# Gates of the first two mixers by exponential, addition and reciprocal in place of Silu, and the last outputs' turn three visits later

## What is computed

```python
def dsa_mixer(h, w_in, q_g, k_g, w_out):
    q, k, v, gate, qi, ki, wi = split_cols(h @ w_in, A_WIDTHS)
    q = rope(rms_norm(q.reshape(B, T, N_HEADS, HEAD_DIM), q_g), pos)
    k = rope(rms_norm(k.reshape(B, T, N_KV_HEADS, HEAD_DIM), k_g), pos)
    ...
        p = jax.nn.softmax(logits, axis=-1).astype(v.dtype)
        o = jnp.einsum('bqgrk,bqkgd->bqgrd', p, v_sel)
    ...
    return (jax.nn.silu(gate) * o) @ w_out
```

## Time and profile before

| | us |
|---|---|
| median of 3 runs | 2319.11 (2318.62 to 2319.35) |
| profiled execution | 2317.59 |
| its span | 2316.2 |
| TensorE busy in the span | 2274.4 (98%) |
| VectorE busy | 1328.2 (57%) |
| ScalarE busy | 1158.7 (50%) |

### The profile page before, as it was taken

One profiled execution on the slowest core, in us unless ns is written; L12 is line 12 of the kernel. 1 busy time (PEld: TensorE's weight loads), 2 busy tenths in 40 slices (PEclk: granted clock), 3 DMA queues, 4 the chain that ended last, 5 costly groups with the idle time before them and its releaser, 6 DMA issues.

```text
span 2316.2 us, 28510 instructions
## 1 busy us (share of the span) xinstructions
PE 2274.4 (98%) x11826; PEld 1874.7 (81%) x11826; DVE 1328.2 (57%) x1787; ACT 1158.7 (50%) x1624; POOL 9.6 (0%) x17
## 2 busy tenths in 40 slices
PE   8999999999999999999999999999999999999998
PEld 6888788888788887878788887887888888888886
DVE  5776654666555566575765555655445544554554
ACT  5556654546664564464444555445443344434443
POOL 0000000000000000000000000000000000000000
PEclk9999999999999999999999999999999999999999
DMA  7454445554545553434644445556555556555653
GB/s 266 143 182 145 146 162 185 180 183 147 173 150 193 160 164 126 146 128 157 201 155 162 146 164 185 180 182 206 190 185 190 191 186 195 182 198 186 196 183 109
DMA packets 204497, 400.01 MB, mean 173 GB/s; under 512 B 12688, under 2 KB 12848, under 8 KB 204240
## 3 DMA queue, kind: packets, MB, share of 16 engines
q1 hardware_dynamic: 201920, 390.03, 51.5%
q0 software_dynamic: 1584, 6.16, 0.9%
q10 hardware_dynamic: 864, 2.00, 0.2%
HBM read 396.06 MB, written 2.10 MB: 172 GB/s over the span
## 4 chain that ended last, share of the span: by engine, by line
PE 91%; DVE 4%; ACT 2%; issue 1%; DMA 0%; ACTq 0%; SPq 0%; DVEq 0%
PE ACC L882 28%; PE ACC L884 27%; PE ACC L883 27%; PE TP L444 2%; ACT arena L905 1%; DVE WL L1861 1%; PE TP L489 1%; PE SCPV L481 1%; PE SCPV L498 0%; PE SCPV L499 0%; PE SCPV L497 0%; ACT WH L905 0%; PE SCPV L480 0%; PE TP L469 0%; PE SCPV L646 0%
## 5 line engine op out<-in xcount | busy, mean ns | idle before, releaser
L1861 DVE TENSOR_TENSOR WL<-W,WH 128x1024 fp32r<-128x1024 f32 x740 | 901.1, 1220 | 659.0 <-ACT WH L905 657.4
L905 ACT ACTIVATE WH<-W 128x1024 fp32r<-128x1024 f32 x740 | 781.5, 1057 | 841.9 <-PE ACC L884 838.9
L882 PE MATMUL ACC<-WH,XH 128*128 128x512 f32 x2592 | 1043.8, 403 | 9.8 <-DVE WL L1861 4.0
L884 PE MATMUL ACC<-WH,XL 128*128 128x512 f32 x2592 | 1012.7, 391 | 0.0
L883 PE MATMUL ACC<-WL,XH 128*128 128x512 f32 x2592 | 1010.7, 390 | 0.0
L882 PEld LDWEIGHTS ACC<-WH,XH 128*128 128x128 f32 x2592 | 487.7, 188 | 117.2 <-issue 9.4
L884 PEld LDWEIGHTS ACC<-WH,XL 128*128 128x128 f32 x2592 | 486.9, 188 | 104.8
L883 PEld LDWEIGHTS ACC<-WL,XH 128*128 128x128 f32 x2592 | 488.3, 188 | 93.3 <-issue 1.0
L882 PE MATMUL ACC<-WH,HH 128*128 128x512 f32 x352 | 138.6, 394 | 0.0
L884 PE MATMUL ACC<-WH,HL 128*128 128x512 f32 x352 | 137.1, 389 | 0.0
L883 PE MATMUL ACC<-WL,HH 128*128 128x512 f32 x352 | 137.1, 389 | 0.0
(11 more groups left out here) (268 smaller groups left out, 1238.6 us busy)
## 6 DMA issues: line engine op xcount, KB each, us to landing
W<-in_w_in SPq DMA_DIRECT2D x84, 1024.0 KB, 5.0
W<-in_a_w_in SPq DMA_DIRECT2D x48, 1024.0 KB, 5.1
W<-in_w_ffn_gate SPq DMA_DIRECT2D x44, 1024.0 KB, 5.2
W<-in_w_ffn_up SPq DMA_DIRECT2D x44, 1024.0 KB, 5.2
W<-in_w_ffn_down SPq DMA_DIRECT2D x44, 1024.0 KB, 5.0
W<-in_b_w_in SPq DMA_DIRECT2D x40, 1024.0 KB, 5.1
W<-in_a_w_out SPq DMA_DIRECT2D x16, 1024.0 KB, 5.0
W<-in_b_w_out SPq DMA_DIRECT2D x16, 1024.0 KB, 5.0
```

The lines of the kernel that those rows point to most:

```text
L882: MM(out, hx, WH[:, k, 0:ch.width], start=q == 0 and k == 0, stop=False)
L884: ins = MM(out, lx, WH[:, k, 0:ch.width], start=False, stop=last and k == QK - 1)
L905: return nc.scalar.activation(out, in_, func, **how)
L1861: TT(tiles_of(M.WL[n % 2], ch, half), tiles_of(M.W[n % 4], ch, half), tiles_of(M.WH[n % 2], ch, half).bitcast(F32), ALU.subtract).then_inc ...
```

## The change

The gate chunks are taken out of the banks by Copy. ScalarE then writes exp(-x) of the whole gate, 128x1024, into a new tile M.GE (on the room of an earlier stage's tiles). VectorE adds 1, takes the reciprocal in place, multiplies the gate by it, and then gates the outputs as before. It does so over three visits: addition and reciprocal, product, gating. The turn of the last 512 columns begins at `after(g3) + 5` instead of `+ 2`.

```diff
-        begin(after(l + ".g3") + 2, "turn", "go." + l, 3)
+        begin(after(l + ".g3") + 5, "turn", "go." + l, 3)
...
+    M.GE = cut(16640, TB, CH)
...
+    def gate(l, g):
+
+        if l == "a":
+            act.wait_ge(*at("mask_made"))
+        if g or l == "b":
+            act.wait_ge(*at("gate_made", *((l, g - 1) if g else ("a", NKV - 1))))
+        act.wait_ge(*at("acc_taken_act", f"{l}.g{g}", 1))
+        A(M.GE.rearrange("p t w -> p (t w)"), M.G[g % 2].rearrange("p t w -> p (t w)"), ACT.Exp, scale=-1.0).then_inc(*did("gate_exponentiated", l, g))
+        yield
...
-            out, f = M.G[int(name[1]) % 2][:, t, :], ACT.Silu
+            out, f = M.G[int(name[1]) % 2][:, t, :], ACT.Copy
...
     def gate(l, g):
-        dve.wait_ge(*at("acc_taken_act", f"{l}.g{g}", 1))
+        dve.wait_ge(*at("gate_exponentiated", l, g))
+        TS(M.GE, M.GE, 1.0, None, ALU.add).then_inc(*did("gate_divisor", l, g))
+        dve.wait_ge(*at("gate_divisor", l, g))
+        V.reciprocal(M.GE, M.GE).then_inc(*did("gate_inverse", l, g))
+        yield
+        dve.wait_ge(*at("gate_inverse", l, g))
+        TT(M.G[g % 2], M.G[g % 2], M.GE, ALU.mult).then_inc(*did("gate_made", l, g))
+        yield
+        dve.wait_ge(*at("gate_made", l, g))
         dve.wait_ge(*at("outputs_taken", l, g, GRP - 1))
```

More of the change, by code:

```diff
@@ L1280, in round_up @@
         A(tiles_of(M.WH[n % 2], ch, half), tiles_of(M.W[n % 4], ch, half), ACT.Copy).then_inc(*did("weights_rounded", n, half))
-    tasks = dict(turn=turn, merge_gates=merge_gates, narrow=narrow, squares=squares, roots=roots, keys=keys, queries=queries, attend=attend, index=index, dn_gates=dn_gates, dn_conv=dn_conv,
+    tasks = dict(turn=turn, gate=gate, merge_gates=merge_gates, narrow=narrow, squares=squares, roots=roots, keys=keys, queries=queries, attend=attend, index=index, dn_gates=dn_gates, dn_conv=dn_conv,
                  dn_norms=dn_norms, dn=dn, dn_out=dn_out, compress_turn=compress_turn, compress=compress, nsa_keys=nsa_keys, nsa_attend=nsa_attend)
```

## The result

The changed kernel takes 2366.4 us (2365.0 to 2367.7, 4 runs) beside 2318.9 us (2317.4 to 2319.4, 4 runs) for the one before on the same chip: **ratio 1.021, 95% interval 1.0197 to 1.0223**, slower. Forecast were 2370.3 us and a range of 2348 to 2386.

The account below looks back on a forecast made before the run. TensorE, busy 98% of the span, was taken to bound the kernel. Waits of 41.0 us plus 10.2 us of lost clock, 51.2 us, on the median of 2319.11 gave 2370.3 us, range 2348 to 2386.

Parts of the forecast that it names:

- What goes: On ScalarE, 8 table loads leave each mixer, 16 x 1.28 = 20.5 us of ScalarE time.
- The limit of 7.1 us of waits: TensorE's waits over both mixers' gate stages: removing the loads returns at most 2 x 3.55 us.
- The reciprocal: VectorE's 128x1024 reciprocal at each of 8 gates: 6.8 us, bounds 5.5 and 7.3.
- The tensor-tensor rate as a rival: Wide reciprocal on VectorE takes 1.2 us, the slow narrow rows being a starting cost; 2320.8 us, chance 0.10.
- the eight-pass reading: VectorE's reciprocal makes eight passes a column: 8.7 us, 15.2 us more over 8 gates, 2385.5 us; chance 0.10.
- Gate 0: TensorE's transposition for the next attention head waits behind VectorE's queue: +5.8 us in mixer a, +4.3 in b.
- Gate 1: Head's masks and maxima stand behind reciprocal and product on VectorE, so TensorE waits: +7.5 us in each mixer.
- Gate 2: TensorE waits 2.0 and 0.75 us for weight remainders (WL), less 0.85 for the bank: +1.9, taken as 2.0.
- Gate 3: At the moved turn, TensorE's first transposition of the last outputs waits for the gating: +5.95 us.
- Sum of the waits: TensorE's added waits over four gates: 21.25 us in mixer a, 19.75 in mixer b, together 41.0.
- The clock: TensorE's lowered clock after six new waits of 6 to 8 us: 6 x 1.7 = 10.2 us lost.
- Rival 3: Not slower: wide reciprocal takes 1.2 us, every chain is 5.6 us shorter; +1.7 us, 2320.8 us; chance 0.10.

Follow-up runs that it names:

- the kernel without a gate: Kernel before with Copy for Silu, no exponential, addition, reciprocal or product, and the turn at after(g3) + 5: 2309.3 us, ratio 0.9965.
- the run with `+ 2`: Changed kernel with the turn of the last outputs back at after(g3) + 2: 2375.3 us, ratio 1.0251 to the kernel before.
- the filled kernel: Changed kernel with 163 unread matmuls ahead of TensorE's six long waits: 2356.1 us, ratio 1.0163.
- the kernel with the minimum: Changed kernel with a tensor-tensor minimum of the same shape in the reciprocal's place: 2319.0 us, ratio 1.0005.
- the kernel with the turn alone: Kernel before, Silu kept, with only the turn moved from after(g3) + 2 to + 5: 2319.0 us, ratio 1.0002.
- the kernel in four pieces: Changed kernel with the reciprocal in four pieces of 256 columns over four visits, turn at after(g3) + 8: 2348.2 us, ratio 1.0128.

## Why the prediction was right, step by step

- **What goes.** There are 16 fewer table loads, two for each gate, as the order said. The limit of 7.1 us of waits is right within 0.2 by the kernel without a gate, 7.3; in time the loads are worth 8.2 us there.
- **The reciprocal**, the deciding term: 6.55 us, where 6.8 was taken from one 8-column row and bounded by 5.5 and 7.3. The tensor-tensor rate as a rival has fallen (five times too low). So has the eight-pass reading of the Trainium skill, "VectorE: DVE Perf Modes", section "First, the fixed hardware budget": by it an estimated 8.7 us, and the measurement decides, 6.55. Between 256 and 1024 columns the slope is (6553 - 1739) / 768 = 6.27 ns a column. The addition took 0.695, not 0.75 us. Together this is 0.3 us less for each gate.
- **Gate 0**: the transposition at 274.34, forecast 275.0. Net of the old waits +5.3 and +3.8, forecast +5.8 and +4.3.
- **Gate 1**: +6.97 in both mixers, forecast +7.5.
- **Gate 2**: 1.45 + 0.51 - 0.85 = +1.1 in each, forecast +2.0. This is the term with the largest error for its size: the first wait was taken as 2.0, the second as 0.75 us, and a rounded-up latency was added.
- **Gate 3**: +5.30 in each, forecast +5.95. The old place would have cost 4.1 more by the run with `+ 2`, as follows from three visits of 1.37 us.
- Sum of the waits: 5.3 + 3.8 + 2 x (6.97 + 1.1 + 5.30) = 35.8, by the pages 36.1, forecast **41.0**. Durations explain 2.4 of the 5 us (8 x 0.3). At gate 0 VectorE's start was read 0.3 us too late as well, 258.8 for 258.51. The rest is spread over the links of the chains and is not taken apart.
- **The clock**: 11.4 us of busy time, and 10.3 when the waits are filled, forecast **10.2**. Its mechanism, that the loss follows the waits, is shown by the filled kernel. That the number came so near is luck: it was one loss of 1.7 us from one row, taken six times. The six rows measure 1.4 to 3.0 us, 2.1 in the mean and 12.9 together, and 1.7 us went the other way at a wait that the prediction had not in its sum.
- **Rival 3** gave 2320.8 with a pass of 1.2 us; the kernel with the minimum has 2319.0, the same within what can be measured. Its premise, a wide reciprocal at the tensor-tensor rate, was false; its chains were right. It had +0.2 and -1.3 at gate 0, +1.9 twice, -0.85 twice and +0.35 twice; net of the old waits of 2.5 us the kernel with the minimum shows +0.2 and -1.2, +1.7 twice, -0.85 twice and nothing at the turn, +0.7 in all.

The error of the total, 3.9 us, is thus 5 us too many in waits and 1 too few in the clock: the two errors partly cancel.

## What to carry to other kernels

Ask of an added instruction not what share its engine has left but how long the one instruction is and what stands behind it in program order: at 59% VectorE's load, 6.55 us in one piece made TensorE wait up to 8.00 us at a stage where it needs a new weight remainder every two visits, 2.7 us. Here the inverse did better on ScalarE, where it is two short instructions: exp(-ln(1 + y)) beside exponentials that are there anyway cost two activations of 1.06 us and left waits of 0.2 us. Size an unknown instruction by two rows of the same narrow width, one of a known rate: here 8 columns were enough to forecast 1024 within 4%.

## What the hardware showed that I had not expected

A TensorE wait of some 2.5 us brings the lower clock in one execution and not in another. At mixer a's first gate the kernel before has 1.00 behind such a wait; the kernel with the turn alone, the same program up to there, has 0.63 over 4.00 us, between the levels 2.4 and 1.2 GHz. First the kernel before, then the other:

```profile
257.85 0.30 PE L489 MATMUL TP<-consts,arena 128*128 128x128 f32 x1 [2.49 <-ACT arena L905]
...
257.85:261.85 4.00, 4.00 (x22) 3.47 (x23) 3.42 (x10) 3.97 (x7) 0.00 (x0) 1.00 0.00 0
```

```profile
258.52 0.87 PE L489 MATMUL TP<-consts,arena 128*128 128x128 f32 x3 [2.49 <-ACT arena L905]
...
258.50:262.50 4.00, 3.98 (x16) 3.63 (x17) 3.42 (x10) 3.97 (x7) 0.00 (x0) 0.63 0.00 0
```

The same with the wait from which the prediction took its price, 0.57 before; after:

```profile
1178.68 0.32 PE L753 MATMUL SCPV<-arena 128*32 128x128 f32 x4 [2.25 <-DVE arena L1767]
...
1178.68:1182.68 4.00, 4.00 (x74) 3.07 (x74) 2.12 (x2) 0.60 (x1) 0.00 (x0) 1.00 0.68 228
```

It shows within one execution too. The kernel in four pieces has two waits of 2.61 us at the same transposition of the two mixers, ended at 298.90 and 637.17. The clock behind them:

```profile
298.90:302.90 4.00, 4.00 (x19) 3.37 (x20) 3.99 (x5) 2.25 (x3) 0.00 (x0) 1.00 0.08 31
...
637.17:641.17 4.00, 4.00 (x17) 3.38 (x18) 3.96 (x5) 1.80 (x4) 0.00 (x0) 0.66 0.02 3
```

So a profile's clock behind one short wait is a throw, and a difference of 2 us in TensorE's busy time between two profiled executions is none (2.2 us in the kernel with the turn alone, whose runs are those of the kernel before within the interval). The times of single runs would fit this: of 21 runs of the kernel before on one chip, 15 lie between 2316.3 and 2318.1 us and 6 between 2319.0 and 2319.8. There is no trace of each of these runs, so it is not shown that the clock makes the gap. What decides it for waits of that size stays open.

Short waits can cost as much clock as long ones. In the kernel in four pieces no wait in the gate stages is over 4.1 us, the clock is at 0.50 to 0.66 over 4.00 us behind six of them, and the busy time grew by 12.2 us, where six waits of 5.3 to 8.0 us lost 12.9.
